# Half of the samples' value pages summed by ScalarE and VectorE, beside a TensorE that is always busy

## What is computed

```
s = q . k * scale + bias      # 1024 keys per sample, 8 heads of 128
p = softmax(s)                # the own token is handled apart
o[h, :] = sum over the 1024 tokens t of p[t, h] * v[t, h, :]
```

## Time and profile before

| | |
|---|---|
| median of 3 runs | 2694.39 us (lowest 2693.01) |
| span of the profiled execution, first to last instruction | 2688.8 us |
| busy: TensorE, VectorE, ScalarE, GpSimd | 2662.4, 1541.8, 1092.0, 147.5 us |
| granted TensorE clock, mean over the span | 0.997 |
| moved | 600.08 MB, mean 223 GB/s |

### The profile page before, as it was taken

How to read it: one execution, slowest core, us unless ns; L and a number is a source line. 1 busy time by engine, 2 the same in 40 slices (tenths; PEclk the granted TensorE clock), 3 DMA queues, 4 the chain that set the end, 5 groups by cost and what they waited for, 6 DMA issues and landing times.

```text
span 2688.8 us, 50855 instructions
## 1 busy us (share of the span) xinstructions
PE 2662.4 (99%) x21748; PEld 2590.7 (96%) x21748; DVE 1541.8 (57%) x2442; ACT 1092.0 (41%) x985; POOL 147.5 (5%) x266
## 2 busy tenths in 40 slices
PE   8999999999999999999999999999999999999998
PEld 7899999999999999999998988999999999999998
DVE  4545554555547778876675744365554545555455
ACT  6433333333335433455352444344433333333345
POOL 0000000000000011211211121100000000000000
PEclk9999999999999999999999999999999999999999
DMA  7665555555555799799979899766555555555553
GB/s 267 235 210 186 176 185 182 177 187 177 185 168 175 237 306 299 240 354 392 339 274 334 280 317 320 232 211 198 173 188 175 185 184 177 185 176 186 181 159 115
DMA packets 487449, 600.08 MB, mean 223 GB/s; under 512 B 12608, under 2 KB 447008, under 8 KB 485984
## 3 DMA queue, kind: packets, MB, share of 16 engines
q1 hardware_dynamic: 442512, 456.37, 52.9%
q0 software_dynamic: 35088, 129.74, 13.3%
q10 hardware_dynamic: 9680, 11.54, 1.2%
HBM read 575.16 MB, written 24.53 MB: 223 GB/s over the span
## 4 chain that ended last, share of the span: by engine, by line
PE 96%; DVE 1%; DMA 1%; ACT 1%; issue 1%; DVEq 0%; POOLq 0%; SPq 0%; ACTq 0%
PE PS L554 30%; PE PS L555 29%; PE PS L556 29%; PE PS L1997 1%; PE PS L590 1%; PE PS L592 1%; PE PS L591 1%; DVE splitL L509 1%; DMA raw<-w_gate 1%; ACT splitH L503 1%; PE PS L1760 0%; PE PS L1497 0%; PE PS L1728 0%; PE PS L1242 0%; PE PS L1356 0%
## 5 line engine op out<-in xcount | busy, mean ns | idle before, releaser
L509 DVE TENSOR_TENSOR splitL<-raw,splitH 128x2048 fp32r<-128x2048 f32 (+1 forms) x462 | 1007.5, 2181 | 841.8 <-ACT splitH L503 840.9
L503 ACT ACTIVATE splitH<-raw 128x2048 fp32r<-128x2048 f32 (+1 forms) x462 | 844.4, 1829 | 1493.4 <-PE PS L556 1443.4
L554 PE MATMUL PS<-gH,splitH 128*128 128x264 f32 x3072 | 880.9, 287 | 5.3 <-DVE splitL L509 5.3
L555 PE MATMUL PS<-gL,splitH 128*128 128x264 f32 x3072 | 871.2, 284 | 0.0
L556 PE MATMUL PS<-gH,splitL 128*128 128x264 f32 x3072 | 870.6, 283 | 0.0
L554 PEld LDWEIGHTS PS<-gH,splitH 128*128 128x128 f32 x3072 | 579.3, 189 | 25.0 <-issue 22.9
L555 PEld LDWEIGHTS PS<-gL,splitH 128*128 128x128 f32 x3072 | 579.7, 189 | 0.5 <-issue 0.2
L556 PEld LDWEIGHTS PS<-gH,splitL 128*128 128x128 f32 x3072 | 576.7, 188 | 0.0
L554 PE MATMUL PS<-hH,splitH 128*128 128x264 f32 x1536 | 436.1, 284 | 0.1
L555 PE MATMUL PS<-hL,splitH 128*128 128x264 f32 x1536 | 435.1, 283 | 0.0
L556 PE MATMUL PS<-hH,splitL 128*128 128x264 f32 x1536 | 434.9, 283 | 0.0
(11 more groups left out here) (378 smaller groups left out, 2969.8 us busy)
## 6 DMA issues: line engine op xcount, KB each, us to landing
raw<-ffn_w SPq DMA_DIRECT2D x240, 1024.0 KB, 5.1
raw<-w_in SPq DMA_DIRECT2D x64, 1024.0 KB, 7.2
raw<-w_gate SPq DMA_DIRECT2D x48, 1024.0 KB, 8.0
ring<-cache_k POOLq DMA_DIRECT2D x64, 512.0 KB, 6.0
ring<-cache_v POOLq DMA_DIRECT2D x64, 512.0 KB, 5.8
raw<-ffn_w SPq DMA_DIRECT2D x32, 768.0 KB, 4.8
raw<-w_out SPq DMA_DIRECT2D x16, 1024.0 KB, 5.5
raw<-w_mem_kv SPq DMA_DIRECT2D x15, 1024.0 KB, 6.4
```

The source lines that it names most:

```text
L503: nc.scalar.activation(splitH[:, s, tiles, :], raw[:, u, 0:nk, :], ACT.Copy).then_inc(hi_ready, 1)
L509: nc.vector.tensor_tensor(splitL[:, s, tiles, :], raw[:, u, 0:nk, :], splitH[:, s, tiles, :].bitcast(F32), ALU.subtract).then_inc(split_re ...
L554: nc.tensor.matmul(out, w_hi, H[:, k, 0:n], start=first, stop=False)
L555: nc.tensor.matmul(out, w_hi, L[:, k, 0:n], start=False, stop=False)
```

## The change

The eight samples are shared out. Samples 0, 2, 4, 6 stay on TensorE as before, their pages in pairs at 16 units. Samples 1, 3, 5, 7 go to ScalarE and VectorE: `vAcc` (128 tokens x 1024) gathers, for one sample, the sum over its 8 pages of page x probability, the probability being one number per token (partition) and head. Page 0 is scaled by ScalarE into `vAcc`; pages 2, 4, 6 are scaled by ScalarE in place in the ring and added by VectorE (one addition of 1024 columns); pages 1, 3, 5, 7 are multiplied and added by VectorE in one instruction per head. Two units after the slot of the last page, TensorE multiplies `vAcc` with ones (four matmuls into PSUM bank 7, `pe_value_sum`), which adds up the 128 tokens. The row is copied, turned and picked as before, two units or more after it is made. `USES` lists the vector pages as VectorE's kind of use. A vector page is released at the end of ScalarE's (page 0) or VectorE's work on it.

Beside that, `KEY_AT` changes for units 77 to 97, with the same number of halves in all, three semaphores become one that counts, `branch_done`, and the load of `mvTok` goes from step 76 to step 78 of POOL. The diff, cut to its core:

```diff
+    vAcc = at("vAcc", [BR_W], M_QB + 4608)
...
-              76: 1, 77: 1, 78: 1, 79: 2, 80: 2, 81: 1, 82: 1, 83: 2, 84: 1, 85: 1, 86: 2, 87: 1, 88: 1, 89: 2,
-              90: 1, 91: 1, 92: 2, 93: 2, 94: 1, 95: 1, 96: 2, 97: 2, 98: 1}
+              76: 1, 77: 2, 78: 3, 79: 3, 80: 3, 81: 2, 82: 2, 83: 1, 84: 1, 85: 1, 86: 1, 88: 1, 89: 1,
+              91: 1, 92: 1, 93: 1, 94: 1, 95: 2, 96: 2, 97: 1, 98: 1}
...
-    VALUE_AT = {**{T: (3, 2, 1, 2)[T % 4] for T in range(108, 132)}, **{T: 2 for T in range(132, 140)}}
+    PE_SAMPLES, VEC_SAMPLES = (0, 2, 4, 6), (1, 3, 5, 7)
+    PE_PAIR_AT = (109, 110, 112, 114, 115, 117, 119, 122, 123, 125, 126, 129, 130, 132, 134, 136)
+    VEC_PAGE_AT = (108, 108, 109, 110, 111, 112, 112, 113, 116, 117, 118, 118, 119, 120, 120, 121, 124, 124, 125, 126, 127, 127, 128, 128, 131, 131, 132, 133, 133, 134, 135, 135)
...
+    SUM_AT = {VEC_PAGE_AT[NPAGES * i + NPAGES - 1] + 2: k for i, k in enumerate(VEC_SAMPLES)}
...
+    def act_vec_page(act, k, g):
+
+        s = page_there(act, ("V", k, g))
+        i = VEC_SAMPLES.index(k)
+        if i == 0 and g == 0:
+            act.wait_ge(d_prob, 2)
+        if i and g == 0:
+            act.wait_ge(v_sum, i)
+        for h in range(A_HEADS):
+            page = ring[:, s, h * P:(h + 1) * P]
+            last = nc.scalar.activation(vAcc[:, h * P:(h + 1) * P] if g == 0 else page, page, ACT.Copy,
+                                        scale=DA["L"][:, k, g, h:h + 1])
+        if g == 0:
+            last.then_inc(page_used[s], 1)
+        else:
+            last.then_inc(v_prod, 1)
+
+    def dve_vec_page(dve, k, g):
+
+        page_read(dve, ("V", k, g - 1))
+        s = PAGE_NO["V", k, g] % RING
+        if g % 2 == 0:
+            dve.wait_ge(v_prod, 3 * VEC_SAMPLES.index(k) + g // 2)
+            nc.vector.tensor_tensor(vAcc[:, :], vAcc[:, :], ring[:, s, :], ALU.add).then_inc(page_used[s], 1)
+            return
+        page_there(dve, ("V", k, g))
+        if g == 1:
+            dve.wait_ge(d_prob, 2)
+        for h in range(A_HEADS):
+            acc = vAcc[:, h * P:(h + 1) * P]
+            last = nc.vector.scalar_tensor_tensor(acc, ring[:, s, h * P:(h + 1) * P], DA["L"][:, k, g, h:h + 1], acc,
+                                                  ALU.mult, ALU.add)
+        last.then_inc(page_used[s], 1)
+
+    def pe_value_sum(pe, T, k):
+
+        page_read(pe, ("V", k, NPAGES - 1))
+        pe.wait_ge(row_out, past_rows(ROW_TURN_AT, T))
+        for j in range(4):
+            last = nc.tensor.matmul(PS[32 * j:32 * j + A_HEADS, 7, 2 * P:4 * P], ones[:, 0:A_HEADS],
+                                    vAcc[:, 2 * j * P:2 * (j + 1) * P], start=True, stop=True)
+        last.then_inc(v_sum, 1)
...
-            pe.wait_ge((r_all_done, m_done, a_done)[(T - T_GATE) // 32], 1)
+            pe.wait_ge(branch_done, (T - T_GATE) // 32 + 1)
...
-        if T == 76:
-            pool.wait_ge(r_all_done, 1)
+        if T == 78:
+            pool.wait_ge(branch_done, 1)
             pool.wait_ge(v_sent, 16)
             pool.dma_start(mvTok[:, :, :], scratch["mv"].rearrange("(t p) c -> p t c", p=P)).then_inc(mv_in, 16)
```

More of the change, by code:

```diff
@@ L1615, in uses @@
             at_slot += [(T, 0, ("MV", b, g)) for g in range(2)]
[L1616 to L1620, removed]
+        for T, (k, g0) in PE_PAIRS.items():
+            at_slot += [(T, 0, ("V", k, g)) for g in (g0, g0 + 1)]
+        for T, pages in VEC_PAGES.items():
+            at_slot += [(T, 1, ("V", k, g)) for k, g in pages]
         return sorted(at_slot, key=lambda e: (e[0], e[1]))
@@ L1988, in pe_mem_values, with rows_before @@
             last.then_inc(page_used[s], 1)
+    def rows_before(samples, k):
+        i = samples.index(k)
+        return PAST_ROWS + (ROW_NO[samples[i - 1]] + 1 if i else 0)
+    def act_vec_page(act, k, g):
[35 more added lines that the diff above has]
+        last.then_inc(v_sum, 1)
     def pe_value_page(pe, k, g):
@@ L1999, in pe_value_page, with dve_decode_out @@
         last.then_inc(page_used[s], 1)
-    def dve_decode_out(dve, link, K, done):
+    def dve_decode_out(dve, link, K):
         t = K.t
@@ L2119, in chunk_at, with pe_side @@
         return 42 + 9 * i // 8
-    def pe_side(pe, T, values):
+    def pe_side(pe, T):
         if T == 0:
@@ L2155, in pe_side @@
         pe_heads(pe, KA, T, MOBA, 3, 5)
[L2156 to L2164, removed]
+        if T in ROW_TURN_AT:
+            pe.wait_ge(row_sb, past_rows([t for t, _, _ in ROWS_MADE], T))
+            pe_row_turn(pe, PAST_ROWS + ROW_NO[ROW_TURN_AT[T]])
+        if T in SUM_AT:
+            pe_value_sum(pe, T, SUM_AT[T])
+        if T in PE_PAIRS:
+            k, g0 = PE_PAIRS[T]
+            pe_value_page(pe, k, g0)
+            pe_value_page(pe, k, g0 + 1)
     def pe_heads(pe, K, T, t0, pitch, lag):
@@ L2213, in act_evac, with act_side @@
             copy_evac(act, T)
-    def act_side(act, T, values):
+    def act_side(act, T):
         if T == 0:
@@ L2256, in act_side @@
             act_exps(act, DKA)
[L2257 to L2263, removed]
+        for k, g in VEC_PAGES.get(T, ()):
+            if g % 2 == 0:
+                act_vec_page(act, k, g)
+        if T in PE_PAIRS:
+            k, g0 = PE_PAIRS[T]
+            if g0 == NPAGES - 2:
+                page_read(act, ("V", k, NPAGES - 1))
+                act_row_copy(act, PAST_ROWS + ROW_NO[k])
+        if T in SUM_AT:
+            k = SUM_AT[T]
+            act.wait_ge(v_sum, VEC_SAMPLES.index(k) + 1)
+            act_row_copy(act, PAST_ROWS + ROW_NO[k], 7, 2 * P)
     def dve_evac(dve, T):
@@ L2283, in dve_evac, with dve_side @@
             scaled_evac(dve, qaT, rinv[:, :])(B, c, u // 2)
-    def dve_side(dve, link, T, keys, values):
+    def dve_side(dve, link, T, keys):
         if T == 0:
@@ L2356, in dve_side @@
         dve_heads(dve, link, KA, T, MOBA, 3, 5)
[L2357 to L2363, removed]
+        for k, g in VEC_PAGES.get(T, ()):
+            if g:
+                dve_vec_page(dve, k, g)
+        if T in ROW_TURN_AT:
+            dve_past_row_out(dve, ROW_TURN_AT[T], DA["oS"])
         if T == 141:
             dve.wait_ge(row_out, PAST_ROWS + DEC)
-            dve_decode_out(dve, link, DKA, a_done)
+            dve_decode_out(dve, link, DKA)
         if T_PROJ <= T < T_OUT and T % 2:
@@ L2377, in dve_side @@
             keys += 1
-        return keys, values
+        return keys
     def pool_pages(pool, T):
@@ L2582, in _ @@
                   lambda i, downs: act_next_h(act, 1, G_MIX, i))
-        values = 0
         for T in range(T_END):
@@ L2590, in _ @@
                 act_evac(act, T)
-            values = act_side(act, T, values)
+            act_side(act, T)
         split_ffn(act_split, act, B_FFN2, 1, act_root_between(act, 1), lambda i, downs: act_y(act, i))
@@ L2618, in _ @@
         dve.wait_ge(stored, 96)
-        keys = values = 0
+        keys = 0
         for T in range(T_END):
@@ L2626, in _ @@
                 dve_split(dve, *mid(T + 2))
-            keys, values = dve_side(dve, link, T, keys, values)
+            keys = dve_side(dve, link, T, keys)
         split_ffn(dve_split, dve, B_FFN2, 1, dve_root_between(dve, link, 1),
```

43 lines of the change are left out of this document (28 added, 15 removed).

## The result

The changed kernel takes 2678.81 us in the median of five runs (2675.59 to 2678.98), the kernel before 2693.8 beside it: a ratio of 0.9939, 95% interval 0.9929 to 0.9950. 2677 was predicted, with 2670 to 2690 as the range. A run's time is 2.0 us above its span here (2678.82 for this execution) and 1.7 above it in the kernel before (2692.88 and 2691.2 in one run). So the profiled execution of before, 2688.8, was some 3 us quicker than its kernel's median, and only 1.7 of the prediction's 5.6 us lie around the span.

A forecast was written before the change was run, and what follows sets the result against it. The prediction took TensorE, busy 99% of the span, as the bound. It summed 2688.8 - 14.5 - 4.8 - 1.4 + 3.5 = 2671.6, plus 5.6 for what lies around the span: 2677 us, range 2670 to 2690.

The forecast's parts named there:

- Value reads: TensorE, units 108 to 140: fewer page batches, plus four sums, and fewer weight-stream restarts save 14.5 us.
- New waits: Value stage: TensorE waits for late pages or splits at units 110, 128, 129 and others, 3.5 us, bounds 0 and 12.
- Unit 110: First pair of pages there: slots released later by ScalarE and VectorE make TensorE wait 1.5 us, bounds 0 and 3.
- The splits for units 128 and 129: Vector pages queued ahead of these splits use up the spare time; 1 us of wait for both, bounds 0 and 4.
- Prices: Vector pages: 2.2 us each on ScalarE (bounds 1.6 and 3.4), 1.7 on VectorE (bounds 1.4 and 2.4).
- The stall at unit 92: New key table removes TensorE's 3.10 us idle there and 1.7 lost to the lower clock: 4.8 us less.
- The later `mvTok` load: Memory-value load moved from POOL's step 76 to 78, away from weight loads: 1.4 us less, bounds 0 and 1.8.
- A: Value-page ring turns too slowly, five more places wait like unit 110 and the clock drops once: 2686 us, chance 0.18.
- C: Transfers become the bound between 1552 and 1650, some 4.5 us of the gain lost: 2681.5 us, chance 0.08.
- B: The key-page stall moves to slot 83 or 93 instead of going, 4.8 us stay: 2682 us, chance 0.12.
- D: VectorE's queue blocks on pages, delaying splits and lowering TensorE's clock, 4.8 us each; six events give 2706; chance 0.06.
- E: TensorE's value reads were already hidden, so the change doesn't do what it says: 2690 us, chance 0.04.

The follow-up runs named there:

- e8: The kernel before with its 64 value pages read in 24 batches (3, 2, 3 and none by unit) instead of 32; ratio to before 0.9993.
- e1: The kernel before with the change's new key table alone; ratio to before 0.9980.
- e2: The kernel before with the `mvTok` load moved from step 76 to 78 alone; ratio to before 0.9997.
- e7: The changed kernel with four of TensorE's 16 page pairs one unit later; 2674.63 us, ratio to before 0.9933.
- e5: The changed kernel with half of the vector pages' products left out, so its sums are not the reference's; ratio to before 0.9936.
- e6: The changed kernel with every vector-page product done as two instructions of 64 columns instead of one of 128; ratio to before 0.9987.
- f1: The changed kernel, unchanged, run a second time; 2679.39 us, ratio to before 0.9942.

## Why the prediction was right, and where it was not

*Value reads, -14.5.* Right mechanism, mis-sized: -15.9. The step that failed is "Alone before are 108, 130 and 133 to 139, nine; after ..., four": the restart of the weight stream was counted only for batches alone in a unit. e8 shows 0.32 us a batch and not 0.12, though six of the eight batches that it saves were not alone in their units. With the 0.31 a batch and 0.42 a page that the timetable of the two traces gave before e8 ran, 32 batches in 32 units become pairs and sums in 17 (three sums share a unit with a pair) and 64 pages become 36 in price: 15 x 0.31 + 28 x 0.42 = 16.4, against 15.9 measured.

*New waits, 3.5.* Right in the sum (3.27), half right in the places, so the sum is in part luck. Unit 110 came as worked out: ScalarE's page ended at 1538.0 (predicted 1537.8), VectorE's at 1540.2 (1539.6), the load went out at 1541.7 and the matmul started at 1546.75 (landing predicted at 1546.6). The wait was 0.86 us, for 1.5 foretold. The rows of ScalarE, VectorE and POOL follow; the last names TensorE's reads as what ended the queue's idle time, but by the order of `USES` the slot that this load takes is the one that VectorE's page gave back:

```profile
1535.54 2.44 ACT L2025 ACTIVATE vAcc<-ring,A_L 128x128 f32<-128x128 f32 x8
1538.01 2.19 DVE L2045 SCALAR_TENSOR_TENSOR vAcc<-ring,A_L,vAcc 128x128 f32<-128x128 f32 x8 [0.46 <-ACT vAcc L2025]
1541.70 0.54 POOL L1671 DMA_DIRECT2D ring<-cache_v  x1 [1.98 <-PE PS L2065]
```

The splits for units 128 and 129 held; pages were late there instead. At 129 VectorE's addition stood behind a split and a head's work and ended at 1651.5; its slot's load went out at 1653.0, and the matmul that waited for it began at 1658.06:

```profile
1646.91 2.29 DVE L510 TENSOR_TENSOR splitL<-raw,splitH 128x2048 fp32r<-128x2048 f32 x1
...
1650.29 1.22 DVE L2038 TENSOR_TENSOR vAcc<-vAcc,ring 128x1024 f32<-128x1024 f32 x1
```

*Prices.* ScalarE's page was put at 2.2 and cost 2.44; the Trainium skill's figure (ScalarE: Activation LUTs, What ACT_TABLE_LOAD costs), from which the prediction had worked out 2.35, was nearer (the time by it would be 2677.4 and not 2677.2, which is the forecast's own sum). The copy that was taken as the nearest row has no operand per partition. VectorE's page was put at 1.7 and cost 2.19, near the upper bound.

*The stall at unit 92, -4.8.* Right, -4.9, and e1 shows that the key table alone does it.

*The later `mvTok` load, -1.4.* Not there. The step "At 1332.59 it stood between weight loads" took what stood next to a late block for its cause. In the changed kernel the load goes out at 1350.92, after the stall, and the block for unit 72 is later than before:

```profile
1338.28 1.91 ACT L504 ACTIVATE splitH<-raw 128x2048 fp32r<-128x2048 f32 x1 [6.46 <-DMA raw<-w_gate]
...
1350.92 0.71 POOL L2513 DMA_DIRECT2D mvTok<-scratch_mv  x1
```

e2 is the one trace that speaks for the load: its units 70 to 75 are 1.7 us shorter than before's, but its median is only 0.7 lower. In place of the gain stands what no rival had: in the traces 2.4 us more in units 70 to 75, whose cause and true size are open.

*The sum.* The two stretches that the change works on gave -12.6 - 4.9 = -17.5, and the median fell by 15.0; the 2.5 us between them are not placed. That the prediction's -17.2 is so near to -17.5 is in part luck: the reads gave 1.4 us more than foretold, which made up for the 1.4 of the load that did not come.

*Rivals.* A and C: e7 (1.1 us of waits at other places) and e5 (1.3 with half the products) leave up to 1.3 us to them. B: didn't happen; units 76 to 88 last 72.99 us in both kernels, and 94 to 107 last 61.4. D: no split came late in the changed kernel, and the clock stayed at 1.00 behind the three waits; at e6's price splits came late by 0.8 us in all, and the clock fell, but behind a wait for a page. E: the reads were on the path.

## What to carry to other kernels

Work that interrupts a saturated stream of matmuls costs by the interruption as well as by the piece: count the units that it leaves empty. Work given to idle engines is hidden until it holds a buffer that the busy engine's next load needs; follow the buffer from its release to the next landing, and place the reader behind that. And before a stall of a few us is put down to what stands next to it, look at it in several traces of both kernels: one pair showed 4.4 us, fourteen traces 2.4 in the mean, and the medians of the times 1.4.

## What the runs showed of the hardware

Narrow instructions are dear on both engines: VectorE's products of 128 columns came 0.27 us apart (2.19 for eight), while one addition of 1024 columns took 1.22; with 64 columns, 0.20 apart, the eight became sixteen and the page 3.23. ScalarE went from 2.44 to 3.93, 0.31 and 0.25 an instruction. The Trainium skill (VectorE: DVE Perf Modes, The TRN2 errata) says that both engines pay a fixed cost for each instruction that reads SBUF, whatever its width; these runs agree: half the columns saved only a quarter of an instruction's time on VectorE and a fifth on ScalarE.

TensorE's clock: behind the waits of 0.86, 1.08 and 1.33 us it stayed at 1.00; behind the stall of 4.19 it was granted 0.74 over the next 9.7 us, and in e6, behind a wait of 4.07, 0.71 over 8.7 us:

```profile
1552.30:1561.00 8.70, 8.68 (x55) 7.78 (x56) 5.85 (x20) 3.56 (x9) 1.60 (x3) 0.71 1.04 383
```

Each cost 2.5 us more than itself. The length of a wait doesn't settle the price: 1.87 us in e1 cost no clock and 1.79 in e8 cost 1.7 us; 3.10 in before cost 1.7, and 3.04 in f1 cost 3.1 (0.74 over 12 us).

In the 25 us before the stall of unit 72 the weights' queue (q1) and POOL's (q0) of the changed kernel moved (packets, MB, share of the 16 engines' time):

```profile
q0 software_dynamic: 1805, 6.73, 72.2%
q1 hardware_dynamic: 2660, 2.67, 31.4%
```

POOL's packets are 3.7 KB, those of the weights 1.0 KB, and the weights got 107 of 377 GB/s. The Trainium skill (DMA: Bandwidth & Descriptors, Queues, rings and completion order) says that an engine takes its queues in turn, a whole packet at a time, by which the queue with the small packets would get the small share. That fits these rows if the profile's packets are the packets meant there, and no run here tests it.
